# One bias row per quarter spread by a shuffle, and another order at the end of routing

## The chip, the cores and the metric

The kernel runs on one NeuronCore of a Trainium2 chip. The metric is the device time of one execution in microseconds; lower is better. A core has five engines that run their own instruction streams and meet at semaphores: TensorE (PE), VectorE (DVE), ScalarE (ACT), GpSimd (POOL) and SyncE (SP, which here only issues transfers). All transfers run on the core's 16 DMA engines.

## The reference

One decoder layer on 1024 tokens of width 1024: adaLN modulation, a gated MLP mixer beside a sparse attention, then a mixture of experts, then a final norm. The change lies in the mixture of experts and in the routing ahead of it:

```python
def moe(h, w_router, b_router, w_gu, b_gu, w_dn, b_dn):
    ...
    logits = (hf @ w_router + b_router).astype(jnp.float32)
    top_logits, top_idx = lax.top_k(logits, TOP_K)          # 4 of 32 experts
    wts = jax.nn.softmax(top_logits, axis=-1)
    ...
    def expert_block(args):
        xb, e = args
        gu = xb @ w_gu[e] + b_gu[e]
        x_glu = jnp.minimum(gu[:, 0::2], SWIGLU_LIMIT)
        x_lin = jnp.clip(gu[:, 1::2], -SWIGLU_LIMIT, SWIGLU_LIMIT)
        act = x_glu * jax.nn.sigmoid(SWIGLU_ALPHA * x_glu) * (x_lin + 1.0)
        return act @ w_dn[e] + b_dn[e]
    ...
```

All data are float32. An expert's weights are 8 MB (gate and up) and 4 MB (down).

## The kernel before

**Stages.** The first 600 us hold the modulation, the projections and the attention. From about 601 us the routing stage walks over 8 tiles of 128 tokens: output projection, residual, norm, transpose, router logits, top 4, and the place of each (token, expert) pair in a list in DRAM (`list_d`), written by indirect transfers of POOL (`scatter`). In the trace this is L1188 to L1520.

**Experts.** From about 738 us the experts run. The tokens of an expert are cut into blocks of 32 (`BLK`). The 128 partitions hold a block four times: partition q*32 + r stands for quarter q of the columns and row r of the block. `up` (L1701) multiplies a block by the gate-and-up weights in two halves h (5 and 3 of 8 column tiles), `gates` (L1754 to L1764, DVE, with the activation of ACT, L1748, in its midst) makes the gated product and transposes it into `actT`, `down` (L1713) multiplies by the down weights, `weigh` (L1776, L1780) adds the down bias and the token's weight. POOL fetches the next block's rows (`gather`, L1650) and adds a finished block to the result in DRAM (`add_rows`, L1659). A block takes PE about 10.4 us.

**Order of the experts.** Experts are placed by their counts from the first tiles: `SEGMENTS` runs through a large expert's first half, a small expert, the large one's second half, for 8 pairs, then 16 middling experts one after another: 40 segments, 143 blocks in all. Every engine reads a segment's number of blocks from memory and loops.

**Weights.** `expert_loads` has SP load each expert in 12 pieces into a ring that holds two experts. A piece is issued when the same piece of the expert two places before is spent and at most `UNDER_WAY` = 4 pieces are under way. Where blocks are many, the ring waits for PE; where they are few, PE waits for the ring.

**Biases.** `b_e` are two tiles of 128 x 768: a quarter's gate, up and down biases (768 numbers) are needed on the 32 partitions of that quarter. `load_bias` has ACT's queue load four transfers of 32 partitions, each reading one row of DRAM 32 times: 4 x 96 KB an expert, 12.6 MB in all. Experts use the two tiles in turn, and a tile is loaded when the expert that used it is through.

**End of routing.** Blocks 0 and 1 (`FIRST` = 2) are known after 4 tiles and are gathered early. After the last tile POOL scatters the last pairs, loads the first expert's whole list (`load_rows`, four transfers of 32 partitions with the same 32 rows), adds block 0 to the result, takes the ids (`take_rows`), gathers block 2, loads the second expert's list, and enters its loop, whose first gather is block 3. PE does `up` of block 0 between the last tiles' products, waits for `halves` (DVE's count of blocks by expert), then does both parts of `down` of block 0, then block 1. DVE does the gates of block 0 after the last places.

## Time and profile before

| what | us |
|---|---|
| median of 3 runs | 2314.43 (2310.81 to 2315.14) |
| the profiled execution's own time | 2316.25 |
| its span, first to last instruction | 2314.4 |
| PE busy | 2200.6 (95%) |
| DVE / POOL / ACT busy | 1029.5 / 849.1 / 333.1 |
| moved by DMA | 534.03 MB, 498.27 MB of it read from HBM |

The profile lists groups of instructions, waits and timelines. "Idle before" is the time in which an engine stood still ahead of an instruction, with the event that ended it. A row of a timeline merges instructions of one line; in brackets stands the idle time ahead of it. PE's ends are modelled. TensorE's clock has two levels, 1.2 and 2.4 GHz; the granted clock is given as a share of the upper one.

### The profile page before, as it was taken

What the parts mean: (1) busy time and instruction counts of PE and PEld (TensorE: products, weight loads), DVE (VectorE), ACT (ScalarE), POOL (GpSimd) and SP (SyncE); (2) the same over time, 40 slices, a digit from 0 to 9 for tenths busy, and PEclk for the clock granted to TensorE, in tenths of its full rate; (3) what the DMA queues carried; (4) which work ended last, traced back from release to release, by engine and by line L of the source; (5) the groups of instructions that cost most, each with busy time, mean ns of one, the idle gap of its engine ahead of it and who ended that gap; (6) DMA issues with size and microseconds to landing.
All of it is one profiled execution on the core that took longest, in us unless ns stands there. A gap on an engine that the chain in (4) does not pass through costs nothing.

```text
span 2314.4 us, 80327 instructions
## 1 busy us (share of the span) xinstructions
PE 2200.6 (95%) x31685; PEld 1502.2 (65%) x31685; DVE 1029.5 (44%) x3487; ACT 333.1 (14%) x919; POOL 849.1 (37%) x1658
## 2 busy tenths in 40 slices
PE   6999989999899899999999999999999999999995
PEld 2777776666544467777777777767675567775573
DVE  2464237777255434343434343434443344443344
ACT  0000017777211000000000000000000000000001
POOL 2011006554224443434343434344443344443433
PEclk9999998999999999999999999999999999999998
DMA  9531051000336787686768686878979978989996
GB/s 312 191 137 58 12 158 35 1 2 1 116 107 229 275 289 250 218 282 224 274 220 287 215 286 213 289 253 276 380 250 355 377 272 317 381 305 390 390 379 224
DMA packets 183488, 534.03 MB, mean 231 GB/s; under 512 B 30152, under 2 KB 59216, under 8 KB 183248
## 3 DMA queue, kind: packets, MB, share of 16 engines
q1 hardware_dynamic: 143472, 479.09, 55.7%
q0 software_dynamic: 33360, 39.96, 8.2%
q10 hardware_dynamic: 6480, 12.72, 1.9%
q8 instruction: 99, 1.62, 0.3%
q14 instruction: 77, 0.63, 0.1%
HBM read 498.27 MB, written 33.34 MB: 230 GB/s over the span
## 4 chain that ended last, share of the span: by engine, by line
PE 55%; DMA 14%; issue 2%; SPq 1%; POOL 1%; DVE 1%; POOLq 0%; another core or an unknown queue 0%; ACT 0%; DVEq 0%; ACTq 0%
PE psum L1701 34%; PE psum L1713 17%; DMA w_ring<-in_w_gate_up 8%; DMA w_ring<-in_w_down 4%; PE psum L1259 4%; DMA x_gathered<-h_rows,scalars_i 1%; SPq L1583 0%; DVE x L1399 0%; POOL slot_list L1214 0%; DMA x<-x_rows 0%; PE psum L1268 0%; DMA token<-k_pairs 0%; SPq L1145 0%; DMA x_rows<-y_out,scalars_i 0%; SPq L1608 0%
## 5 line engine op out<-in xcount | busy, mean ns | idle before, releaser
L1701 PE MATMUL psum<-w_ring,xT 128*32 128x320 f32 (+1 forms) x18304 | 1023.7, 381 | 19.2 <-issue 14.7
L1701 PEld LDWEIGHTS psum<-w_ring,xT 128*32 128x32 f32 x18304 | 696.6, 110 | 340.7 <-issue 41.5
L1713 PE MATMUL psum<-w_ring,actT 128*32 128x256 f32 x9152 | 531.0, 382 | 17.3 <-DMA w_ring<-in_w_down 15.7
L1713 PEld LDWEIGHTS psum<-w_ring,actT 128*32 128x32 f32 x9152 | 349.8, 111 | 152.6 <-DMA w_ring<-in_w_down 20.7
L1642 POOL TENSOR_TENSOR scalars<-scalars 128x1 f32<-128x1 f32 x575 | 108.9, 189 | 728.8 <-DVE xT L1768 562.6
L1754 DVE TENSOR_TENSOR glu<-psum,expert_bias 128x160 f32<-128x160 f32 (+1 forms) x286 | 83.1, 291 | 537.8 <-PE psum L1701 537.7
L1748 ACT ACTIVATE glu<-glu 128x160 f32<-128x160 f32 (+1 forms) x286 | 88.7, 310 | 1444.3 <-DVE glu L1756 1429.7
L1659 POOL DMA_INDIRECT x_rows<-y_out,scalars_i x142 | 228.0, 1606 | 47.2 <-issue 46.9
L783 POOL TENSOR_SCALAR scores<-scores,coef 128x64 f32<-128x64 f32 (+5 forms) x128 | 134.1, 1063 | 137.5 <-DVE coef L992 137.5
L1650 POOL DMA_INDIRECT x_gathered<-h_rows,scalars_i x144 | 153.3, 1064 | 81.3 <-issue 79.2
L1776 DVE TENSOR_TENSOR psum<-psum,expert_bias 128x256 f32<-128x256 f32 x143 | 61.8, 432 | 242.2 <-PE psum L1713 223.4
L906 ACT ACTIVATE scores<-scores,nmax 128x64 f32<-128x64 f32 (+8 forms) x192 | 114.5, 600 | 15.3 <-DVE nmax L977 15.0
L1780 DVE SCALAR_TENSOR_TENSOR y_out<-psum,scalars,gate_q 128x256 f32<-128x256 f32 x143 | 69.1, 483 | 76.9 <-DMA x_rows<-y_out,scalars_i 63.5
L977 DVE CUSTOM_DVE_ANT_0 scores<-psum,attn_tables 128x512 f32<-128x512 f32 (+4 forms) x192 | 81.5, 462 | 38.3 <-PE psum L831 38.0
L849 PEld LDWEIGHTS psum<-ident,scores 128*128 128x128 f32 (+1 forms) x592 | 62.5, 139 | 49.0 <-issue 41.2
L1764 DVE STREAM_TRANSPOSE actT<-lin 128x160 f32<-128x160 f32 (+1 forms) x286 | 89.2, 312 | 10.0
L849 PE MATMUL psum<-ident,scores 128*128 128x128 f32 (+1 forms) x592 | 90.4, 286 | 0.9 <-ACT probT L915 0.6
L1762 DVE SCALAR_TENSOR_TENSOR lin<-lin,glu 128x160 f32<-128x160 f32 (+1 forms) x286 | 83.6, 292 | 11.2 <-ACT glu L1748 0.7
L831 PE MATMUL psum<-kT_all,q_negated 64*128 64x512 f32 (+3 forms) x384 | 84.4, 522 | 1.4 <-DVE nmax L977 0.6
L329 POOL TENSOR_TENSOR vms<-vms,eps 128x8 f32<-128x8 f32 x8 | 5.6, 706 | 215.7 <-DVE vms L582 215.7
L1620 POOL DMA_DIRECT2D slot_rows<-slot_list x128 | 67.3, 541 | 43.5 <-issue 43.5
L915 ACT COPY probT<-psum 128x512 f32<-128x512 f32 (+1 forms) x136 | 74.2, 572 | 55.4 <-PE psum L849 45.0
(246 smaller groups left out, 1882.7 us busy)
## 6 DMA issues: line engine op xcount, KB each, us to landing
w_ring<-in_w_gate_up SPq DMA_DIRECT2D x128, 1280.0 KB
w_ring<-in_w_down SPq DMA_DIRECT2D x128, 1024.0 KB
w_ring<-in_w_gate_up SPq DMA_DIRECT2D x128, 768.0 KB
ada_then_cmp_in<-in_w_ada SPq DMA_DIRECT2D x16, 1024.0 KB, 6.3
expert_bias<-bias_by_quarter ACTq DMA_DIRECT2D x128, 96.0 KB
ada<-in_w_ada SPq DMA_DIRECT2D x8, 1024.0 KB, 5.6
xt<-in_x SPq DMA_DIRECT2D x8, 512.0 KB, 6.3
w_uv_then_w_out<-in_w_in SPq DMA_DIRECT2D x4, 1024.0 KB, 9.5
```

Of the source, the lines that this page charges most:

```text
L783: nc.gpsimd.tensor_scalar(rows, rows, coef[qt % 2][:, col:col + 1], None, ALU.mult).then_inc(s_sl, 1)
L831: last = nc.tensor.matmul(psA[at % 2][g][:, col:col + m], qn[qt % 2][half(g), j, :], keys, start=True, stop=True)
L849: last = nc.tensor.transpose(psT[at % 2][0:m, (2 * t + g) * P:(2 * t + g + 1) * P], score[n % (LAG + 1)][g][:, c0:c0 + m], ident[:])
L906: nc.scalar.activation(rows, rows, ACT.Exp, scale=-1.0, bias=nmax[qt % 2][:, col:col + 1], accum_out=sums[qt % 2][:, col:col + 1]).then_in ...
L1259: last = nc.tensor.matmul(psO[n], mix, wo[:, k, n * 512:(n + 1) * 512], start=(k == 0), stop=(k == KD - 1))
L1642: nc.gpsimd.tensor_tensor(tick[:], zero[:], zero[:], ALU.add).then_inc(s_steps, 1)
L1650: nc.gpsimd.indirect_dma_start(xg[:], None, h2_q, bass.IndirectOffsetOnAxis(ap=ids_x[:], axis=0), bounds_check=4 * (SEQ + BLK) - 1, oob_is ...
L1659: nc.gpsimd.indirect_dma_start(x1_q, bass.IndirectOffsetOnAxis(ap=ids_y[:], axis=0), y_out[:], None, compute_op=ALU.add).then_inc(s_ysc, 16)
L1701: last = nc.tensor.matmul(psU[h][j * BLK:(j + 1) * BLK, :], xT[:, k, :], w[:, j], start=(k == 0), stop=(k == KD - 1))
L1713: last = nc.tensor.matmul(psO[m * BLK:(m + 1) * BLK, :], actT[h][:, i, :], w[:, m * Q:(m + 1) * Q], start=(k == 0), stop=(k == KD - 1))
L1748: nc.scalar.activation(glu[:, 0:n], glu[:, 0:n], ACT.Gelu_apprx_sigmoid).then_inc(s_gate[h], 1)
L1764: nc.vector.transpose(actT[h][:].rearrange("p k q -> p (k q)"), lin[h][:]).then_inc(s_actT[h], 1)
```

## The change

It has these parts. (1) `load_bias` loads one row to the first partition of each quarter, 4 x 3 KB, and a new `spread_bias` has DVE copy it to the other 31 partitions by one STREAM_SHUFFLE over 128 x 768 in place, once an expert: before the loop of the expert's first segment, and for expert 0 in the routing stage. Both tiles are cleared once by POOL. (2) The list rows come in one transfer to 128 partitions, whose source names the 32 rows four times, in place of four transfers. (3) POOL computes the address of the first expert's list ahead of the last scatter, and gathers block 2 ahead of adding block 0. (4) DVE and ACT do the first half of block 0's gates right after the loop over tiles, and PE its part of `down` ahead of the `halves` products.

```diff
                 parts.gather(pool, 1, 4)
         tiles(pool, body)
         scatter(TILES - 2, 0)
+        lines = parts.lines_of(pool, 0)
         scatter(TILES - 1, 1)
         for i in range(2):
             pool.wait_ge(s_sc[i], 16 * TOPK * TILES // 2)
             pool.wait_ge(s_xnst[i], 16 * TILES // 2)
-        parts.load_rows(pool, 0)
+        parts.load_lines(pool, 0, lines)
         pool.wait_ge(s_spare, 48)
         for i in range(2):
             pool.wait_ge(s_x1st[i], 16 * TILES // 2)
-        parts.add_rows(pool, 0, 7)
         parts.take_rows(pool, 0)
         pool.wait_ge(parts.s_ids, 4)
-        parts.gather(pool, 2, 10)
+        parts.gather(pool, 2, 7)
+        parts.add_rows(pool, 0, 10)
         parts.load_rows(pool, 1)
         pool.wait_ge(s_order, 3)
         expert_rows(pool, parts)
...
         places(TILES - 1, 1)
 
         nc.tensor.matmul(psR[0:E, E:E + 2], total_b[0][:], ones[:, 0:2], start=True, stop=True).then_inc(s_cnt, 1)
+        pe.wait_ge(parts.s_actT[0], 1)
+        parts.down(pe, 0, 0)
         pe.wait_ge(s_halves, 1)
         for i in range(2):
             last = nc.tensor.matmul(psR[0:1, P + i * E:P + (i + 1) * E], halves[:, i:i + 1], select[0:E, :], start=True,
                                     stop=True)
         last.then_inc(s_cnt, 1)
-        parts.down_both(pe, 0, 0)
+        pe.wait_ge(parts.s_actT[1], 1)
+        parts.down(pe, 0, 1)
         pe.wait_ge(parts.s_xT, 3)
         parts.up(pe, 0, 0)
         parts.up(pe, 0, 1)
...
             if back:
                 weights(t - 1, 1 - par)
         tiles(act, body)
+        parts.activation(act, 0, 0)
         copy_h2(TILES - 1, 1)
         copy_logits(TILES - 1)
         weights(TILES - 1, 1)
-        for b in range(FIRST):
-            parts.activations(act, b)
+        parts.activation(act, 0, 1)
+        parts.activations(act, 1)
         act.wait_ge(s_order, 3)
         expert_activations(act, parts)
         final_squares(act, final)
...
             if t == KNOWN_TILES + 1:
                 place_experts()
         tiles(dve, body)
+        parts.spread_bias(dve, 0)
+        parts.gates(dve, 0, 0, 0)
         assign(TILES - 2, 0)
         choose(TILES - 1, 1)
         assign(TILES - 1, 1)
...
         nc.vector.tensor_scalar(none[:], key[0:1, 0:1].to_broadcast([1, N_SEGMENTS]), 0.0, None, ALU.mult)
         with nc.allow_low_precision("whole numbers up to 16"):
             nc.vector.tensor_reduce(halves[:], over[:].rearrange("p (j i) -> p i j", i=2), AX.X, ALU.add).then_inc(s_halves, 1)
-        dve.wait_ge(parts.s_bias[0], 64)
-        parts.gates(dve, 0, 0, 0)
         parts.gates(dve, 0, 1, 0)
         parts.transpose_x(dve, 1)
         dve.wait_ge(s_cnt, 4)
...
         which = pool.value_load(order[0:1, e:e + 1], min_val=0, max_val=E - 1)
         return list_v[bass.ds(which, 1)].rearrange("a t l -> (a t) l")
 
+    def load_lines(pool, e, lines):
+        pool.dma_start(rows_f[e % 2][:].rearrange("p b c -> p (b c)"), lines.partition_broadcast(4)).then_inc(s_rows, 16)
+
     def load_rows(pool, e):
-        lines = lines_of(pool, e)
-        for q in range(4):
-            pool.dma_start(rows_f[e % 2][q * BLK:(q + 1) * BLK, :, :].rearrange("p b c -> p (b c)"), lines
-                           ).then_inc(s_rows, 16)
+        load_lines(pool, e, lines_of(pool, e))
 
     def load_first_rows(pool):
         lines = lines_of(pool, 0)
-        for q in range(4):
-            pool.dma_start(rows_f[0][q * BLK:(q + 1) * BLK, 0:FIRST, :].rearrange("p b c -> p (b c)"), lines[:, 0:2 * FIRST]
-                           ).then_inc(s_rows, 16)
+        pool.dma_start(rows_f[0][:, 0:FIRST, :].rearrange("p b c -> p (b c)"), lines[:, 0:2 * FIRST].partition_broadcast(4)
+                       ).then_inc(s_rows, 16)
 
     def clear(pool):
         nc.gpsimd.memset(zero[:], 0.0).then_inc(s_clear, 1)
...
         nc.gpsimd.memset(xg[:], 0.0).then_inc(s_xT, 1)
 
         nc.gpsimd.memset(tick[:], 0.0).then_inc(s_steps, 1)
-        pool.wait_ge(s_clear, 3)
+        for i in range(2):
+            nc.gpsimd.memset(b_e[i][:], 0.0).then_inc(s_clear, 1)
+        pool.wait_ge(s_clear, 5)
         pool.wait_ge(s_c, 16)
 
     def carry_waits(pool, done):
...
                                      compute_op=ALU.add).then_inc(s_ysc, 16)
 
     def take_first_rows(pool):
-        pool.wait_ge(s_rows, 64)
+        pool.wait_ge(s_rows, 16)
         nc.gpsimd.tensor_tensor(rows_f[0][:, 0:FIRST, 0], rows_f[0][:, 0:FIRST, 0], quarter[:, 0:1].to_broadcast([P, FIRST]), ALU.add
                                 ).then_inc(s_quarter, 1)
         pool.wait_ge(s_quarter, 1)
...
             skip = skip + FIRST
         pool.wait_ge(s_ids, 2 * g + 2)
         if part != 1:
-            pool.wait_ge(s_rows, 64 * (e + 2))
+            pool.wait_ge(s_rows, 16 * (e + 2))
             nc.gpsimd.tensor_tensor(rows_f[e % 2][:, :, 0], rows_f[e % 2][:, :, 0], quarter[:, 0:1].to_broadcast([P, EDGES]), ALU.add
                                     ).then_inc(s_quarter, 1)
         pool.wait_ge(s_quarter, e + 2)
...
             act.wait_ge(s_y, blocks)
         rows = bias_d.rearrange("(e q) n -> e q n", q=4)[bass.ds(which, 1)].rearrange("a q n -> (a q) n")
         for q in range(4):
-            act.dma_start(b_e[at][q * BLK:(q + 1) * BLK, :], rows[q].partition_broadcast(BLK)
-                          ).then_inc(s_bias[at], 16)
+            act.dma_start(b_e[at][q * BLK:q * BLK + 1, :], rows[q:q + 1, :]).then_inc(s_bias[at], 16)
+
+    def spread_bias(dve, p):
+
+        at = HALF_OF[p]
+        turn = sum(HALF_OF[q] == at for q in range(p + 1))
+        dve.wait_ge(s_bias[at], 65 * turn - 1)
+        nc.vector.stream_shuffle(b_e[at][:], b_e[at][:], mask=[0] * BLK).then_inc(s_bias[at], 1)
+        dve.wait_ge(s_bias[at], 65 * turn)
 
     def load_gate(act):
         for q in range(4):
...
                                                                             ).partition_broadcast(BLK)
                           ).then_inc(s_g, 16)
 
+    def activation(act, b, h):
+        act.wait_ge(s_glu[h], b + 1)
+        n = ACT_TILES[h] * BLK
+        nc.scalar.activation(glu[:, 0:n], glu[:, 0:n], ACT.Gelu_apprx_sigmoid).then_inc(s_gate[h], 1)
+
     def activations(act, b):
         for h in range(2):
-            act.wait_ge(s_glu[h], b + 1)
-            n = ACT_TILES[h] * BLK
-            nc.scalar.activation(glu[:, 0:n], glu[:, 0:n], ACT.Gelu_apprx_sigmoid).then_inc(s_gate[h], 1)
+            activation(act, b, h)
 
     def gates(dve, b, h, at):
         n, first, end = ACT_TILES[h] * BLK, 2 * BLK * ACT_FROM[h], 2 * BLK * (ACT_FROM[h] + ACT_TILES[h])
...
         b = parts.first_of(dve, g)
         many = parts.many_of(dve, g)
         dve.wait_ge(parts.s_ids, 2 * g + 4)
-        e = SEGMENTS[g][0]
+        e, part = SEGMENTS[g]
         at = HALF_OF[e]
-        dve.wait_ge(parts.s_bias[at], 64 * sum(HALF_OF[p] == at for p in range(e + 1)))
+        if g and part != 1:
+            parts.spread_bias(dve, e)
         with dve.Fori(0, many) as i:
             n = b + i
             parts.gates(dve, n, 0, at)
```

A last hunk, left out here, only makes the new functions known to the callers.

How instructions stand on DVE after the loop over tiles, before (weights of the last tile but one, `wts`, then its places, `prod` and `rank_f`; the waits in brackets name semaphores):

```order
L1424 CAST mask_b<-mask 128x32
L1426 RECIPROCAL winv<-wsum 128x1 [waits wexp_ready]
L1427 TENSOR_SCALAR wts<-wexp,winv 128x4 [waits dve_chain3]
L1433 TENSOR_TENSOR prod<-hot,psum 128x128 [waits place_ps,dve_chain3]
L1434 TENSOR_REDUCE rank_f<-prod 128x4 [waits dve_chain3]
L1435 CAST rank<-rank_f 128x4 [waits dve_chain3]
```

and in the change:

```order
L1431 RECIPROCAL winv<-wsum 128x1 [waits wexp_ready]
L1432 TENSOR_SCALAR wts<-wexp,winv 128x4 [waits dve_chain3]
L1747 STREAM_SHUFFLE expert_bias<-expert_bias 128x768 [waits expert_bias_loaded0,dve_chain3]
L1770 TENSOR_TENSOR glu<-psum,expert_bias 128x160 [waits w_spent3,expert_bias_loaded0]
L1772 TENSOR_SCALAR glu<-glu 128x160 [waits gates_chain]
L1773 TENSOR_TENSOR lin<-psum,expert_bias 128x160
L1775 TENSOR_SCALAR lin<-lin 128x160 [waits gates_chain]
L1778 SCALAR_TENSOR_TENSOR lin<-lin,glu 128x160 [waits gate_ready0,gates_chain]
L1780 STREAM_TRANSPOSE actT<-lin 128x160 [waits gates_chain]
L1438 TENSOR_TENSOR prod<-hot,psum 128x128 [waits place_ps]
L1439 TENSOR_REDUCE rank_f<-prod 128x4 [waits dve_chain3]
```

The shuffle and six instructions of the gates of block 0 now stand between the weights and the places.

ACT at the same place, before, from the last residual's square (`sq`) to the first activation (`glu`):

```order
L1354 ACTIVATE sq,ms_1<-x 128x1024 [waits rstd3_ready,ms3_ready,x1_ready]
L1368 ACTIVATE wexp,wsum<-below_top 128x4 [waits neg_top_ready]
L1359 COPY h2T<-psum 128x512 [waits xnT_ps]
L1359 COPY h2T<-psum 128x512
L1364 COPY logitsT_parts<-psum 128x128 [waits logitsT_ps]
L1368 ACTIVATE wexp,wsum<-below_top 128x4 [waits neg_top_ready]
L1748 ACT_TABLE_LOAD
L1748 ACTIVATE glu<-glu 128x160 [waits glu_ready0]
L1748 ACTIVATE glu<-glu 128x96 [waits glu_ready1]
```

and in the change:

```order
L1358 ACTIVATE sq,ms_1<-x 128x1024 [waits rstd3_ready,ms3_ready,x1_ready]
L1372 ACTIVATE wexp,wsum<-below_top 128x4 [waits neg_top_ready]
L1760 ACT_TABLE_LOAD
L1760 ACTIVATE glu<-glu 128x160 [waits glu_ready0]
L1363 COPY h2T<-psum 128x512 [waits xnT_ps]
L1363 COPY h2T<-psum 128x512
L1368 COPY logitsT_parts<-psum 128x128 [waits logitsT_ps]
L1372 ACT_TABLE_LOAD
L1372 ACTIVATE wexp,wsum<-below_top 128x4 [waits neg_top_ready]
L1760 ACT_TABLE_LOAD
L1760 ACTIVATE glu<-glu 128x96 [waits glu_ready1]
```

The first activation, with a table load, stands ahead of the copy of the last tile's transposes (`h2T`), and two more table loads have come in.

POOL from the load of the first expert's list (`slot_rows`) on, before:

```order
L1620 DMA slot_rows<-slot_list 32x64 x4
L1642 TENSOR_TENSOR scalars<-scalars 128x1 [waits y_sb,x1_stored1,index_steps,x1_stored0,spare_rows_set]
L1657 TENSOR_TENSOR scalars_i<-row_ids,scalars_i 128x1
L1642 TENSOR_TENSOR scalars<-scalars 128x1 [waits index_steps]
L1659 DMA x_rows<-y_out,scalars_i 4224x256
L1681 TENSOR_TENSOR slot_rows<-slot_rows,quarter 128x32 [waits slot_rows_loaded,ids_ready]
L1684 CAST row_ids<-slot_rows 128x14 [waits quarter_added]
L1685 COPY slot_weights<-slot_rows 128x14
L1642 TENSOR_TENSOR scalars<-scalars 128x1 [waits index_steps,xT_ready,ids_ready]
L1648 TENSOR_TENSOR scalars_i<-row_ids,scalars_i 128x1
L1642 TENSOR_TENSOR scalars<-scalars 128x1 [waits index_steps]
L1650 DMA x_gathered<-h_rows,scalars_i 128x256
```

and in the change:

```order
L1623 DMA slot_rows<-slot_list 128x1x64
L1687 TENSOR_TENSOR slot_rows<-slot_rows,quarter 128x32 [waits ids_ready,x1_stored1,slot_rows_loaded,x1_stored0,spare_rows_set]
L1690 CAST row_ids<-slot_rows 128x14 [waits quarter_added]
L1691 COPY slot_weights<-slot_rows 128x14
L1648 TENSOR_TENSOR scalars<-scalars 128x1 [waits index_steps,xT_ready,ids_ready]
L1654 TENSOR_TENSOR scalars_i<-row_ids,scalars_i 128x1
L1648 TENSOR_TENSOR scalars<-scalars 128x1 [waits index_steps]
L1656 DMA x_gathered<-h_rows,scalars_i 128x256
L1648 TENSOR_TENSOR scalars<-scalars 128x1 [waits index_steps,y_sb]
L1663 TENSOR_TENSOR scalars_i<-row_ids,scalars_i 128x1
L1648 TENSOR_TENSOR scalars<-scalars 128x1 [waits index_steps]
L1665 DMA x_rows<-y_out,scalars_i 4224x256
```

The gather of block 2 (`x_gathered`) now comes ahead of the addition of block 0 to the result (`x_rows`), the load of the list is one transfer to 128 partitions, and the load of the second expert's list follows the addition in place of the gather.

## Rows read from the trace of the kernel before

**Rows 1.** Waits of PE in 1740:1755, 1820:1833, 2080:2092, 2120:2163 (us, times, longest)

```profile
PE psum L1713 <- DMA w_ring<-in_w_down: 3.3, 2, 1.9
...
PE psum L1713 <- DMA w_ring<-in_w_down: 3.9, 2, 2.6
...
PE psum L1713 <- DMA w_ring<-in_w_down: 3.7, 2, 2.1
...
PE psum L1713 <- DMA w_ring<-in_w_down: 4.6, 3, 1.6
```

**Rows 2.** Timeline of PE, the first products after three of those waits

```profile
1752.29 7.09 PE L1701 MATMUL psum<-w_ring,xT 128*32 128x320 f32 x128
...
1831.41 8.74 PE L1701 MATMUL psum<-w_ring,xT 128*32 128x320 f32 x128
...
2090.13 9.08 PE L1701 MATMUL psum<-w_ring,xT 128*32 128x320 f32 x128
```

**Rows 3.** Timeline of SP, where three unbroken stretches of weight loads begin

```profile
1707.52 22.25 SPq L1608 DMA_DIRECT2D w_ring<-in_w_gate_up  x8
...
1784.89 22.86 SPq L1608 DMA_DIRECT2D w_ring<-in_w_gate_up  x8
...
2044.05 23.39 SPq L1608 DMA_DIRECT2D w_ring<-in_w_gate_up  x8
```

**Rows 4.** Timeline of ACT, bias loads inside those stretches

```profile
1739.11 1.76 ACTq L1734 DMA_DIRECT2D expert_bias<-bias_by_quarter  x4
...
1817.21 2.87 ACTq L1734 DMA_DIRECT2D expert_bias<-bias_by_quarter  x4
...
2146.01 1.84 ACTq L1734 DMA_DIRECT2D expert_bias<-bias_by_quarter  x4
```

**Rows 5.** DMA queues in the window 2044:2160 us (packets, MB, share of 16 engines)

```profile
q1 hardware_dynamic: 9951, 38.57, 87.1%
...
q10 hardware_dynamic: 768, 1.57, 4.7%
```

**Rows 6.** Timeline of DVE about the start of a segment at 1063 us

```profile
1068.05 0.33 DVE L1754 TENSOR_TENSOR glu<-psum,expert_bias 128x160 f32<-128x160 f32 x1 [3.73 <-PE psum L1701]
...
1069.56 0.35 DVE L1764 STREAM_TRANSPOSE actT<-lin 128x160 f32<-128x160 f32 x1
...
1072.09 0.40 DVE L1768 STREAM_TRANSPOSE xT<-x_gathered 128x256 f32<-128x256 f32 x1
```

**Rows 7.** Timeline of POOL at the start of the routing stage

```profile
606.63 0.10 POOL L1195 MEMSET eps_nhalf<- 128x1 f32 x1 [3.05 <-DMA quarter<-k_quarter]
```

**Rows 8.** Timeline of DVE at the end of routing

```profile
748.38 0.29 DVE L1433 TENSOR_TENSOR prod<-hot,psum 128x128 f32<-128x128 f32 x1 [3.07 <-PE psum L1293]
...
756.86 0.29 DVE L1433 TENSOR_TENSOR prod<-hot,psum 128x128 f32<-128x128 f32 x1 [3.26 <-remote]
```

**Rows 9.** Timeline of ACT at the end of routing

```profile
746.53 1.07 ACT L1359 COPY h2T<-psum 128x512 f32<-128x512 f32 x2 [2.83 <-PE psum L1268]
...
751.74 1.28 ACT L1748 ACT_TABLE_LOAD   x1
```

**Rows 10.** Timeline of POOL at the end of routing

```profile
768.03 2.07 POOL L1620 DMA_DIRECT2D slot_rows<-slot_list  x4 [3.78 <-issue]
...
771.99 0.92 POOL L1681 TENSOR_TENSOR slot_rows<-slot_rows,quarter 128x32 f32<-128x32 f32 x1
...
774.73 1.09 POOL L1650 DMA_INDIRECT x_gathered<-h_rows,scalars_i  x1 [0.56 <-issue]
...
782.52 1.09 POOL L1650 DMA_INDIRECT x_gathered<-h_rows,scalars_i  x1 [0.56 <-issue]
```

**Rows 11.** The chain that ended last, POOL's address load (start, us)

```profile
766.77 0.31 POOLq L1614
```

**Rows 12.** Timeline of PE from the end of routing on

```profile
759.51 0.21 PE L1330 MATMUL psum<-select,half_counts 32*1 32x32 bf16 x2 [5.84 <-DVE half_counts L1500]
...
790.08 7.12 PE L1701 MATMUL psum<-w_ring,xT 128*32 128x320 f32 x128 [0.85 <-DVE xT L1768]
```

2 lines of the change are left out of this document (added).

## Prediction

> **What bounds the kernel now.** I read the page first: PE is busy 95% of the span, so time is to be had only where PE stands still. So I took the waits of PE from 790 us on. Up to 1700 us the only wait for data is one of 0.85 us, at 790.08 [rows 12]. After that PE waits for the pieces of the down weights in four places: 3.3, 3.9, 3.7 and 4.6 us, 15.5 us in all [rows 1]. Next come the products that follow: 128 products take 7.09 us after the first wait, but 8.74 and 9.08 us after the second and third [rows 2], so there the clock's fall costs 1.6 and 2.0 us more.
>
> Then the timeline of SP: its weight loads run without a gap from 1707.52, from 1784.89 and from 2044.05 us, each time released by PE [rows 3]. The first stretch ends at the first wait, the second at the second, the third holds the third and fourth waits. In such a stretch whatever else the DMA engines carry delays the last piece, and PE with it. The bias loads are such a thing: two are issued in each of the first two stretches (the second ones at 1739.11 and 1817.21) and four in the third, the last at 2146.01 [rows 4], all ahead of the wait that ends the stretch. The DMA queues in 2044:2160 show their part: q10, which carries only them, moved 1.57 MB and took 4.7% of the 16 engines' time [rows 5].
>
> The other place is the end of routing. PE gets block 3 only at 790.08, 0.85 us after it was free [rows 12]; the chain to it runs over DVE's last places, POOL's last scatter, the list rows, and the gathers at 774.73 and 782.52 [rows 10].
>
> **The biases, what is saved.** One expert's biases take 4.7% of 116 us over 4 = 1.36 us of all DMA engines. By bytes it is less: 0.39 MB at q1's rate (87.1% of 116 us for 38.57 MB, 2.62 us/MB) is 1.03 us [rows 5]. After the change 4 rows in place of 128 move, one part in 32. The shares of the queues add up to over 100%, so the first figure is a little high; I take 1.2 us per expert, bounds 1.03 and 1.36.
>
> First stretch: 2 x 1.2 = 2.4 of the 3.3 us. Second: 2.4 of the 3.9, and with 1.5 us left I also take back the 1.6 us of the clock, as 3.3 us of waiting in two pieces cost no clock at 1752.29 [rows 2]: 4.0. Third: 4 x 1.2 = 4.8 of 8.3; the 2.0 us of clock are not added, since they lie between two waits for the same unbroken stretch: what PE gains there it waits at the next. Stretches begin when PE has spent a piece, so an earlier PE shifts the next stretch along and the gains add up. Sum 2.4 + 4.0 + 4.8 = **11.2 us**; bounds 8.2 (1.03, no clock) and 12.5 (1.36, with it). Elsewhere the DMA engines wait for PE, and fewer bytes give nothing.
>
> **The shuffle, what it costs.** 31 segments get one, ahead of DVE's wait for PE. The trace has no shuffle. The nearest row is a transpose, 0.40 us for 256 elements a partition and 0.35 for 160 [rows 6]: 768 elements are at least 0.40 + 512 x 0.52 ns = 0.67 us, at most 3 x 0.40 = 1.2 us. I take 1.0. It costs nothing: DVE stands still 3.73 us at the start of a segment until PE's first half of `up` is done [rows 6]. Part of those are its two address loads; the first instruction of such a load takes 0.31 us on POOL [rows 11], so some 2 us of cover are left. Without the cover it is 31 us. What is queued behind it is the segment's first gates, for which ACT and then PE's `down` wait; the next gather's transpose comes only after them. The bias rows are issued a segment or more ahead, as before. The Trainium skill, "VectorE: DVE Perf Modes", the perf-mode table, gives a shuffle about 2400 ns for 2048 elements, so 0.9 us here as its estimate; no row shows one.
>
> Clearing the two bias tiles adds two memsets to POOL at the stage's start, where it stands still 3.05 us for a constant anyway [rows 7]: nothing.
>
> **The end of routing.** (a) DVE is free at 745.31 (748.38 less its idle 3.07) [rows 8]. The shuffle ends at 746.3, two operations like the 0.33 us of [rows 6] end at 746.95, and the activation, taken as one more of them, at 747.3. ACT now does it ahead of copying the last tile's transposes, which started at 746.53 [rows 9]. That copy feeds the logits, the last places and the last scatter: **+0.8 us** on the whole chain. DVE's own places, waited for until 748.38, are hardly late. The two added table loads are 1.28 us each [rows 9]; the one ahead of the exponential has the logits' product and DVE's reduction as cover: nothing. (b) The list's address is known before the last scatter: the load it saves begins with 0.31 us [rows 11]; I take -0.5 for both instructions and what hangs on them. (c) Four issues of 2.07 us together become one. A quarter is 0.52, an indirect issue for 128 rows 1.09; I take 0.8: -1.3. (d) The list landed at most 1.9 us after the last issue ended (770.10 to 771.99) [rows 10]. Its 128 pieces now hang on one transfer. I take +0.5, bounds 0 and a second 1.9. So the gather of block 2 moves by 0.8 - 0.5 - 1.3 + 0.5 = -0.5 us. PE is there in time: half of block 0's `down` now fills the 5.84 us that PE stood still before 759.51 [rows 12].
>
> But block 3 decides. Between the two gathers POOL now also has the addition of block 0 (1.9 us, it stood ahead of 771.99 [rows 10]), one issue for four (-1.3) and again the landing (+0.5): its gather moves by -0.5 + 1.9 - 1.3 + 0.5 = **+0.6 us**, PE's 790.08 too. Both of PE's gains ahead of it turn into waiting. SP's first loads of expert 1 wait for that addition as well and begin later; blocks of expert 0 cover them. Bounds: -0.9 with the cheap ends, +4.0 with the dear ones. Below that lies one more: at 756.86 DVE ends a wait of 3.26 us whose releaser the profile doesn't know [rows 8], in the midst of this chain. If it doesn't come again, 3.3 us less: -4.2.
>
> For (d) a rule speaks against the change. The row shows only a list spread over 32 partitions by transfer. The Trainium skill, "DMA: Bandwidth & Descriptors", rules for kernel authors, says that an outermost dimension that repeats the source c times confines a transfer to at most c DMA engines: here 4. By it the landing would be near the dear end at both lists.
>
> **Sum.** -11.2 + 0.6 = -10.6 us. The profiled execution took 2316.25 us, which gives 2305.65. It lies 1.8 above the median of the runs shown, 2314.43, so I forecast 2303.8.
>
> **Rivals.**
> 1. *The bias rows sit on one DMA engine.* A piece is ready when the slowest engine is. Before, 768 packets for four experts were 12 an engine and expert [rows 5]; 4 rows of 3 KB in packets of 2 KB (1.57 MB over 768) are 8 packets. All on one engine save it only 4 of 12, 0.4 us an expert: 0.8 + 0.8 + 1.6 - 0.6 = 2.6 us, 2311.8. For it: a transfer with one partition has nothing to be spread by. Against: the row may be cut.
> 2. *Nothing is saved*, since the same row read 32 times was cheap and the weights are held up elsewhere: 2315.0. Against: q10's share of engine time [rows 5] is dearer per byte than q1's.
> 3. *The lists land late*, both by the dear ends: -11.2 + 4.0 = -7.2, 2307.2. The skill's rule above is this rival's.
> 4. *The unexplained wait doesn't come again*: -10.6 - 3.3, 2300.5.
> 5. *Slower: the shuffle is not covered.* Place: a segment's start on DVE. It decides when shuffle and address loads last over 3.73 us. Were all of it on the path: +31 - 10.6, 2334.8. Against: that idle time is three times the dearest shuffle [rows 6].
>
> **Chances.** Forecast 0.50, rivals 0.15, 0.07, 0.15, 0.08, 0.05. What a measurement of this kernel tells from no change is about 0.2%, 4.6 us. The forecast, rivals 3 and 4 are faster by more, of rival 1 a fifth: 0.76. Same: 0.19. Slower: 0.05. Range 2297.5 (12.5 + 4.2 saved) to 2312.5 (rival 1 and a late list).
>
> **What would show it.** Right: q10's share in the late stretches is near nothing, the four waits shrink from 15.5 to about 6 us, the products after 1831 us take 7.1 us, the STREAM_SHUFFLE lasts 1.0 us and DVE still waits after it, the last `h2T` copy starts 0.8 us later, block 3 at about 790.7. Wrong: waits as long as before with q10 empty (rivals 1, 2), a second gather after 785 us (3), block starts that slip at every new expert (5).

## The result, and the profile after

The changed kernel takes 2296.32 us (median of 6 runs, 2292.22 to 2301.77), the kernel before 2313.44 (6 runs): ratio 0.9925, 95% interval 0.9914 to 0.9935. It is faster by 17.1 us where 10.6 were forecast, and lies 1.2 us below the range. The profiled execution took 2299.49 us (span 2297.6).

**The late stretches.** Waits of PE after the change in 1690:1760, 1760:1860, 2020:2100 and 2100:2170 us, which answer to [rows 1] (us, times, longest):

```profile
PE psum L1707 <- issue: 0.7, 2, 0.4
...
PE psum L1719 <- DMA w_ring<-in_w_down: 0.8, 1, 0.8
...
PE psum L1719 <- DMA w_ring<-in_w_down: 1.0, 1, 1.0
...
PE psum L1719 <- DMA w_ring<-in_w_down: 4.5, 3, 1.6
```

The first place has no wait for data left (its 0.7 us are of another kind, marked "issue"), the second and third have shrunk from 3.9 and 3.7 us, and the fourth is as long as before. Next come the products after the second and third place, and the last of the three waits of the fourth:

```profile
1821.21 7.09 PE L1707 MATMUL psum<-w_ring,xT 128*32 128x320 f32 x128
...
2074.50 7.09 PE L1707 MATMUL psum<-w_ring,xT 128*32 128x320 f32 x128
...
2142.13 1.93 PE L1719 MATMUL psum<-w_ring,actT 128*32 128x256 f32 x16 [1.47 <-DMA w_ring<-in_w_down]
```

7.09 us answer to 8.74 and 9.08 in [rows 2]; in 1820:1833 and 2085:2100 the granted clock was 0.80 and 0.77 before, and is 1.00 after. The clock had cost more than that: in the kernel before, 16 products of the down product behind the waits ran slowly too, 1.94 us where 1.07 is the full pace:

```profile
1827.18 1.28 PE L1713 MATMUL psum<-w_ring,actT 128*32 128x256 f32 x16 [2.62 <-DMA w_ring<-in_w_down]
1829.70 1.94 PE L1713 MATMUL psum<-w_ring,actT 128*32 128x256 f32 x16 [1.24 <-DMA w_ring<-in_w_down]
...
2088.42 1.94 PE L1713 MATMUL psum<-w_ring,actT 128*32 128x256 f32 x16 [1.63 <-DMA w_ring<-in_w_down]
```

The DMA queues of the changed kernel in 2044:2160 us (packets, MB, share of 16 engines), against [rows 5]: q10 went from 4.7% to nothing, q1 carries 3.45 MB more in the same time.

```profile
q1 hardware_dynamic: 11001, 42.02, 92.1%
...
q10 hardware_dynamic: 32, 0.05, 0.1%
```

The price of a bias load is best read from SP, which in the third stretch issues without a gap, so that from one expert's first load to the next's is what an expert costs the DMA engines. First load of the stretch and of the fourth expert behind it, before (the first is in [rows 3]) and after:

```profile
2185.59 2.85 SPq L1608 DMA_DIRECT2D w_ring<-in_w_gate_up  x2
```

```profile
2032.14 22.33 SPq L1613 DMA_DIRECT2D w_ring<-in_w_gate_up  x8
...
2167.84 19.77 SPq L1613 DMA_DIRECT2D w_ring<-in_w_gate_up  x7
```

Before (2185.59 - 2044.05) / 4 = 35.4 us per expert, after (2167.84 - 2032.14) / 4 = 33.9: 1.46 us per load, where 1.2 was taken and 1.36 was the upper bound. In the rest of this text "the expert's period" is this number.

**Where the time went.** The start of each block after against before: 2.6 us earlier at block 4, 2.0 to 2.1 from block 30 to block 93, 5.7 behind the first stretch's wait, 11.9 behind the second, 17.6 behind the third, 17.6 behind the fourth, 18.0 at the last. So 15.9 us lie in the late stretches (3.7 + 6.0 + 5.8, and 0.4 elsewhere), 2.0 ahead of them; the kernel's end gives 1.2 back.

**Block 0.** Behind the 2.0 us stands a gain that nobody looked for, where a bias load meets the gather of block 0. ACT issues expert 1's biases at 727.15 before and at 726.59 after, and POOL the gather at 730.96 and 730.37. DVE's transpose of the gathered rows and PE's first products of block 0, before, then after:

```profile
737.75 0.45 DVE L1768 STREAM_TRANSPOSE xT<-x_gathered 128x256 f32<-128x256 f32 x1 [0.59 <-DMA x_gathered<-h_rows,scalars_i]
738.25 6.20 PE L1701 MATMUL psum<-w_ring,xT 128*32 128x320 f32 x64 [2.41 <-DVE xT L1768]
```

```profile
736.55 0.44 DVE L1784 STREAM_TRANSPOSE xT<-x_gathered 128x256 f32<-128x256 f32 x1
737.04 4.51 PE L1707 MATMUL psum<-w_ring,xT 128*32 128x320 f32 x64 [1.73 <-DVE xT L1784]
```

Before, DVE waits 0.59 us for the rows; after, they are there. PE's wait is 0.7 us shorter, and the same 64 products take 1.7 us less: the granted clock in 738.3:744.3 was 0.72, and is 1.00 after. Together that is 2.4 us. All 20 kernels of this study side with their bias load: from the start of these products to PE's next operation it is 4.4 us in the ten that load one row or 192 B pieces, and 6.1 to 6.5 us in the ten that load more.

**The shuffle**, at the start of a segment (idle time ahead of a row in brackets), and as a group:

```profile
1062.88 1.03 DVE L1747 STREAM_SHUFFLE expert_bias<-expert_bias 128x768 f32<-128x768 f32 x1
1065.65 0.33 DVE L1770 TENSOR_TENSOR glu<-psum,expert_bias 128x160 f32<-128x160 f32 x1 [1.74 <-PE psum L1707]
...
L1747 DVE STREAM_SHUFFLE expert_bias<-expert_bias 128x768 f32<-128x768 f32 x32 | 33.4, 1045 | 0.3
```

**The end of routing**, POOL, then PE, DVE and ACT (idle time ahead of a row in brackets):

```profile
762.21 0.78 POOL L1623 DMA_DIRECT2D slot_rows<-slot_list  x1 [2.41 <-DMA slot_list<-pairs,slot]
764.81 0.39 POOL L1687 TENSOR_TENSOR slot_rows<-slot_rows,quarter 128x32 f32<-128x32 f32 x1 [1.83 <-DMA slot_rows<-slot_list]
...
766.84 1.12 POOL L1656 DMA_INDIRECT x_gathered<-h_rows,scalars_i  x1 [0.55 <-POOL scalars L1648]
...
769.82 1.41 POOL L1623 DMA_DIRECT2D slot_rows<-slot_list  x1
775.07 0.23 POOL L1687 TENSOR_TENSOR slot_rows<-slot_rows,quarter 128x32 f32<-128x32 f32 x1 [3.84 <-DMA slot_rows<-slot_list]
...
777.34 1.10 POOL L1656 DMA_INDIRECT x_gathered<-h_rows,scalars_i  x1 [0.55 <-issue]
...
747.50 0.64 PE L1278 MATMUL psum<-h2T,w_router_sb 128*32 128x128 f32 x16 [3.34 <-ACT h2T L1363]
...
785.20 9.36 PE L1707 MATMUL psum<-w_ring,xT 128*32 128x320 f32 x128 [4.39 <-DVE xT L1784]
...
752.19 0.29 DVE L1438 TENSOR_TENSOR prod<-hot,psum 128x128 f32<-128x128 f32 x1
...
746.15 0.34 ACT L1760 ACTIVATE glu<-glu 128x160 f32<-128x160 f32 x1 [2.29 <-DVE glu L1772]
746.39 1.05 ACT L1363 COPY h2T<-psum 128x512 f32<-128x512 f32 x2
```

The gather of block 2 comes 7.9 us earlier (766.84 for 774.73), that of block 3 only 5.2 (777.34 for 782.52). DVE's wait of 3.26 us without a known releaser [rows 8] is absent at 752.19. PE runs ahead over blocks 0 to 2 and then stands still 4.39 us for block 3, and the product behind takes 9.36 us in place of 7.12 [rows 12]: of the 8.4 us won at block 2, 2.6 are left at block 4.

### The profile page after: what moved, and what is told of

The parts are those of the page before. It is cut to its first block, busy times and chain, and to the rows that moved or that the text cites. A ratio compares the mean times of both kernels' runs of the same rounds, so it can differ in the third digit from the quotient of the medians.

```text
span 2297.6 us, 80188 instructions
## 1 busy us (share of the span) xinstructions
PE 2194.2 (96%) x31685; PEld 1501.2 (65%) x31685; DVE 1062.1 (46%) x3551; ACT 335.5 (15%) x921; POOL 807.2 (35%) x1561
## 4 chain that ended last, share of the span: by engine, by line
PE 58%; DMA 11%; issue 1%; SPq 1%; POOL 1%; DVE 1%; POOLq 0%; ACT 0%; DVEq 0%; ACTq 0%
PE psum L1707 36%; PE psum L1719 18%; DMA w_ring<-in_w_gate_up 7%; PE psum L1260 4%; DMA w_ring<-in_w_down 3%; POOL slot_list L1214 0%; DVE x L1404 0%; SPq L1588 0%; DMA slot_rows<-slot_list 0%; DMA x<-x_rows 0%; DMA x_gathered<-h_rows,scalars_i 0%; PE psum L1269 0%; DMA token<-k_pairs 0%; SPq L1145 0%; DMA x_rows<-y_out,scalars_i 0%
## 5 line engine op out<-in xcount | busy, mean ns | idle before, releaser
L783 POOL TENSOR_SCALAR scores<-scores,coef 128x64 f32<-128x64 f32 (+5 forms) x128 | 134.1, 1063 | 137.5 <-DVE coef L992 137.5
L1773 DVE TENSOR_TENSOR lin<-psum,expert_bias 128x160 f32<-128x160 f32 (+1 forms) x286 | 81.0, 283 | 0.0
## 6 DMA issues: line engine op xcount, KB each, us to landing
w_ring<-in_w_down SPq DMA_DIRECT2D x128, 1024.0 KB, 10.4
```

Source lines behind the costliest of these rows:

```text
L783: nc.gpsimd.tensor_scalar(rows, rows, coef[qt % 2][:, col:col + 1], None, ALU.mult).then_inc(s_sl, 1)
```

## The experiments

All were timed against the kernel before on the same chip. One line each; the edits follow (waits of semaphores that go with an edit are left out). Every ratio has its own kernel before, whose median lay between 2313.3 and 2315.3 us. "16 pieces of 192 B", "16 copies, 8 partitions apart" and "16 different rows, neighbouring" compute another result: they leave biases out or add wrong ones.

```
kernel                                     median us  ratio   95% interval      expert's period
bias change alone                          2291.96    0.9899  0.9886 to 0.9911  33.4
all but the bias change                    2318.97    1.0020  1.0011 to 1.0028  35.8
list in four transfers                     2295.27    0.9920  0.9907 to 0.9933  33.8
16 copies of a row                         2316.25    1.0016  1.0005 to 1.0027  35.4
second transfer, 31 copies                 2682.26    1.1581  1.1560 to 1.1602
second transfer, 31 different rows         2680.00    1.1573  1.1553 to 1.1592
POOL's old order                           2294.47    0.9913  0.9897 to 0.9929  33.5
old order of PE, ACT and DVE               2295.56    0.9920  0.9904 to 0.9936  33.9
second transfer, 16 different rows         2324.39    1.0049  1.0033 to 1.0065  35.3
second list early                          2293.39    0.9912  0.9898 to 0.9926  33.9
second list early, engines' old order      2295.00    0.9920  0.9907 to 0.9933  33.6
four shuffles                              2349.53    1.0152  1.0137 to 1.0167
one transfer of 128 rows                   2371.10    1.0246  1.0231 to 1.0262
16 pieces of 192 B per quarter             2299.86    0.9938  0.9924 to 0.9952  33.9
4 copies of a row                          2300.65    0.9947  0.9932 to 0.9962  34.2
bias change and one transfer per list      2294.32    0.9915  0.9903 to 0.9928  33.7
16 copies, 8 partitions apart              2305.78    0.9960  0.9946 to 0.9973  34.7
16 different rows, neighbouring            2316.80    1.0011  1.0002 to 1.0020  35.3
```

### Bias and routing apart

The bias change alone (against the kernel before):

```diff
-            act.dma_start(b_e[at][q * BLK:(q + 1) * BLK, :], rows[q].partition_broadcast(BLK)
-                          ).then_inc(s_bias[at], 16)
+            act.dma_start(b_e[at][q * BLK:q * BLK + 1, :], rows[q:q + 1, :]).then_inc(s_bias[at], 16)
...
-        dve.wait_ge(parts.s_bias[0], 64)
+        parts.spread_bias(dve, 0)
         parts.gates(dve, 0, 0, 0)
```

> Only the bias rows and the shuffle are changed against the kernel before; the lists and the order at the end of routing are as before. Theory A (the biases are worth more than the 11.2 us of the prediction: all 15.9 us by which the block starts shift at the three late stretches hang on them): 2313.4 - 15.9 = 2297.5 us. Rival B (the biases give the 11.2 us forecast, and the other 4.7 us at the stretches come from the lists, which cost one issue on POOL per expert in place of four and one transfer in place of four): 2302.2 us, and the waits of PE for w_down after 1700 us keep about 5 us more than in the changed kernel. Rival C (the two changes help each other only together): above 2305 us.

2291.96 us, 21.7 faster than its kernel before (2313.62) and 4.4 faster than the whole change, with intervals that don't meet. Theory A's sign was right and its size too small; B and C fall. Its four waits after 1700 us are 0, 0, 0 and 3.6 us. The last is the only one left:

```profile
PE psum L1715 <- DMA w_ring<-in_w_down: 3.6, 3, 1.8
```

The same edit taken back in the changed kernel:

> The changed kernel with the bias loads of before and no shuffle: the lists and the end of routing alone. Theory A: it loses the 15.9 us again, 2296.3 + 15.9 = 2312.2 us, with four waits for w_down of together about 15 us after 1700 us and the products at half clock behind the second and third. Rival B: 2296.3 + 11.2 = 2307.5 us, with the waits about 4 to 5 us shorter than before. The prediction's own figure for this part was slower by 0.6 than before, so 2314.0 us; the block starts up to block 93 say 2 us faster.

2318.97 us: slower than before by 0.1 to 0.3%, so the rest of the change is no gain but a loss of 4.4 us with the bias change and 5.4 without it. Theory A's 2312.2 is passed, B falls.

```diff
-        pool.dma_start(rows_f[e % 2][:].rearrange("p b c -> p (b c)"), lines.partition_broadcast(4)).then_inc(s_rows, 16)
+        for q in range(4):
+            pool.dma_start(rows_f[e % 2][q * BLK:(q + 1) * BLK, :, :].rearrange("p b c -> p (b c)"), lines
+                           ).then_inc(s_rows, 16)
```

> The changed kernel with each list loaded by four transfers of 32 partitions as before; everything else as changed. Theory A: only the end of routing moves: four issues for one cost 1.3 us before each of the two gathers, the landing is up to 1.4 us shorter (2.35 in place of 3.84 us at the second list), so between 0 and +2 us: 2296.3 to 2298.5 us, and no waits for w_down come back after 1700 us. Rival B: 4.7 us of the waits come back: 2301 to 2303 us. By the landing's dear end (the one transfer costs more than the four issues it saves) it is faster than the changed kernel by up to 1 us.

2295.27 us: as the changed kernel within the intervals, so no gain or loss of the one transfer for four is seen; the intervals leave room for 2 us either way.

### What a bias load costs by

```diff
-            act.dma_start(b_e[at][q * BLK:q * BLK + 1, :], rows[q:q + 1, :]).then_inc(s_bias[at], 16)
+            act.dma_start(b_e[at][q * BLK:q * BLK + 16, :], rows[q].partition_broadcast(16)).then_inc(s_bias[at], 16)
```

> The changed kernel with each bias row loaded to 16 partitions of its quarter in place of 1 (before: 32), the shuffle unchanged: half of the bytes and descriptors of before. If the cost goes by the bytes (theory A), half of the 15.9 us comes back: 2296.3 + 8.0 = 2304.3 us; by the prediction's 11.2 us half is 5.6: 2301.9 us. If the pieces of w_down have slack first (a wait begins only when the slack is used up) it is less than half: about 2299 to 2301 us, with the first stretch's wait near 1 us and no products at half clock. If the shuffle and not the bytes mattered, or if one row's four transfers sat on one DMA engine and were a cost themselves, 2296.3 or less.

2316.25 us: half of the bytes cost nearly all of it (19.9 of 22.7 us). The prediction's price, which goes by the bytes or the packets' own time, falls here. The trace has each DMA packet with its time, which led to the next idea: the weight packets beside a load are slower while it runs.

The next two kernels keep the one-row load and add a second transfer per quarter:

```diff
             act.dma_start(b_e[at][q * BLK:q * BLK + 1, :], rows[q:q + 1, :]).then_inc(s_bias[at], 16)
+            act.dma_start(b_e[at][q * BLK + 1:(q + 1) * BLK, :], rows[q].partition_broadcast(BLK - 1)).then_inc(s_bias[at], 16)
```

The second kernel has `bias_d[q * BLK:(q + 1) * BLK - 1, :]` as the source.

> The changed kernel with a second transfer per quarter that fills its other 31 partitions with copies of the same bias row, 8 transfers per expert; the shuffle writes over them, so the result is the same and the bytes are those of before again. Theory H (a row that many DMA engines read at the same time slows the packets of the weights beside it: 253 to 278 ns for a weight packet of 5120 B in the 4 us after a bias load begins, against 200 ns else): as with the loads of before, 2316 to 2321 us, with such packets again at 250 ns and more. Theory by bytes alone: 2296.3 + 11 to 16 = 2307 to 2312 us.

> The same as the kernel beside it, but the 31 partitions of a quarter get 31 different rows of the bias tensor (fixed ones), so bytes, packets and transfers are equal and only the addresses differ. Theory H: what is left is the packets' own time, 124 of about 0.12 us over 16 engines = 0.95 us per expert against some 2.0 for the copies, so about half the loss: 2304 to 2309 us, and weight packets of 5120 B stay near 205 ns during the load. Theory by bytes or packets: the same time as the kernel beside it, within 2 us.

2682 and 2680 us, some 385 slower than the changed kernel; no theory had this, and the runs say nothing on copies. ACT's timeline at the end of a segment shows the cause:

```profile
859.28 0.24 ACTq L1741 DMA_DIRECT2D expert_bias<-bias_by_quarter  x1
859.68 7.50 ACTq L1740 DMA_DIRECT2D expert_bias<-bias_by_quarter  x1
867.27 0.50 ACTq L1741 DMA_DIRECT2D expert_bias<-bias_by_quarter  x1
869.30 0.34 ACT L1761 ACTIVATE glu<-glu 128x160 f32<-128x160 f32 x1 [17.26 <-issue]
```

The seventh issue of an expert takes 7.50 us, and ACT's engine stands still for 17.26 us ahead of the activation behind it, which the block's down product needs. Each transfer of 31 rows has one 4-byte packet (its signal) in the trace, where those of 16 and of 32 rows have 16. The Trainium skill, "DMA: Bandwidth & Descriptors", "Why a DMA increments its semaphore by 16 and not by 1", says that as many DMA engines take part as the largest number up to 16 that divides the slowest dimension of both sides, and that each posts a signal; the trace agrees: 31 rows, one signal; 16 rows, 16. By that rule all 31 rows went through one engine.

```diff
             act.dma_start(b_e[at][q * BLK:q * BLK + 1, :], rows[q:q + 1, :]).then_inc(s_bias[at], 16)
+            act.dma_start(b_e[at][q * BLK + 16:(q + 1) * BLK, :], bias_d[q * BLK:q * BLK + 16, :]).then_inc(s_bias[at], 16)
```

> The changed kernel with a second transfer per quarter that brings 16 different rows of the bias tensor to 16 of its other partitions; the shuffle writes over them. Transfers, packets and bytes are those of the kernel that loads the same row to 16 partitions (2316.3 us), and 16 rows spread over 16 engines (31 rows sat on one and cost 386 us), but no row is read twice. Theory H (one row read by 16 engines at once is what is dear, for its own packets, 177 ns against 125, and for the weight packets beside it, 285 to 333 ns against 205): only the packets' own time is left, 64 of 0.125 us and as many of 0.01 over 16 engines = 0.54 us per expert against 1.8, so about 0.3 of the 20 us: 2300 to 2304 us, weight packets of 5120 B near 205 to 220 ns during the load. Theory by bytes or packets: 2314 to 2318 us.

2324.39 us; not the 2300 to 2304 of theory H. But it holds a second cause: with eight issues ACT stands still 18 times, for up to 10.4 us, without a wait that the profile knows (166 us in all, none in the changed kernel), and blocks slip there, mostly by 0.5 to 1 us. Only the late stretches count for the question: 35.3 us per expert, as with copies. H is in doubt.

> The changed kernel with one bias transfer per expert, which brings each of the 4 rows to the 32 partitions of its quarter (one transfer of 128 rows; bytes as before the change, one issue in place of four; the shuffle changes nothing then). Theory K (a bias load costs by transfers times the DMA engines each uses: 64 such pairs before and with 16 rows, 4 now): 16 pairs, a quarter of the loss, 2296.3 + 5 = about 2301 us, 34 to 34.3 us per expert in the late stretches. Theory B (by bytes, but on the busiest engine or with a floor that 16 rows already reach): 2314 to 2318 us as before, 35.4 us per expert.

```diff
-        for q in range(4):
-            act.dma_start(b_e[at][q * BLK:q * BLK + 1, :], rows[q:q + 1, :]).then_inc(s_bias[at], 16)
+        act.dma_start(b_e[at][:], rows.unsqueeze(1).to_broadcast([4, BLK, 3 * D // 4])).then_inc(s_bias[at], 16)
```

2371.10 us: both theories missed it. One transfer whose slowest dimension is 4 has 4 signals in the trace, so by the same rule 4 engines carry 32 rows each, and PE waits 46.9 us for the down weights after 800 us.

> The changed kernel, but a quarter's transfer brings only the first 48 of the row's 768 numbers, to 16 partitions: the biases of the other columns are left out, so the result is another; transfers, packets and engines are those of the kernel with 16 copies (2316.3 us), the bytes are those of one row. Theory K: the loss is as with 16 copies: 2312 to 2318 us, 35.4 us per expert in the late stretches. Theory B: as the changed kernel or a little above, 2296 to 2299 us, since 64 packets of 192 B take 0.03 us each, 0.15 us per engine with their 4 signals.

```diff
+            act.dma_start(b_e[at][q * BLK:q * BLK + 16, 0:48], rows[q][0:48].partition_broadcast(16)).then_inc(s_bias[at], 16)
```

2299.86 us, 3.5 above the changed kernel, with intervals that meet. As many packets, signals and engines as with 16 copies, and nearly nothing of its 20 us: theory K falls.

> The changed kernel with each bias row loaded to 4 partitions of its quarter in place of 1: 16 packets of 3 KB per expert, on up to 4 engines per transfer. Theory K: 16 pairs, a quarter of the loss: about 2301 us. Theory B by total bytes (4 of 32 rows): 2297 to 2299 us. By a floor that any spread transfer reaches: 2310 us and more.

```diff
+            act.dma_start(b_e[at][q * BLK:q * BLK + 4, :], rows[q].partition_broadcast(4)).then_inc(s_bias[at], 16)
```

2300.65 us, 4.3 above: K's figure, which the run with 192 B pieces has refuted as a reason; theory B's 2297 to 2299 is within the noise as well, and only the floor of 2310 falls. What is left is many engines that move 3 KB each at the same time; nothing between 4 and 16 was tried. The last two runs ask whether reading or writing is dear:

```diff
+            first = 4 * (q % 2) + q // 2
+            act.dma_start(b_e[at][first:first + 121:8, :], rows[q].partition_broadcast(16)).then_inc(s_bias[at], 16)
```

> As the kernel with 16 copies of each bias row (2316.3 us), but the 16 partitions that a transfer writes are 8 apart over the whole tile in place of neighbours. Every quarter then takes the biases of the first, so the result is another; transfers, packets, engines, bytes and the rows read are the same. Theory D (what is dear is the writing into a few neighbouring partitions): 2298 to 2303 us, 33.6 to 34.2 us per expert in the late stretches, weight packets of 5120 B below 240 ns. Theory S (what is dear is that 16 engines read one row at once): 2314 to 2318 us, 35.3 us per expert, weight packets at 285 to 330 ns. If neither matters, 2314 to 2318 us here and in the kernel beside it.

```diff
+            act.dma_start(b_e[at][q * BLK:q * BLK + 16, :], bias_d[q * BLK:q * BLK + 16, :]).then_inc(s_bias[at], 16)
```

> As the kernel with 16 copies of each bias row (2316.3 us), with the same 16 neighbouring partitions, but 16 different rows of the bias tensor (fixed ones) in place of copies, so the biases added are others and the result is another; transfers, packets, engines, bytes and the partitions written are the same. Theory D: 2314 to 2318 us. Theory S: 2298 to 2303 us. The run with 16 different rows and eight transfers speaks for D, but there ACT was held up by the eighth issue.

16 different rows on neighbouring partitions: 2316.80, as 16 copies there (2316.25). What is read doesn't matter; theory S falls. 16 copies on partitions 8 apart: 2305.78, 10.5 us less with as many packets of the same size. Where they are written matters, and theory D holds for about half of the loss. The periods say the same (SP, first load of the stretch and of the fourth expert behind it; 35.4 us with 16 copies on neighbours, 34.7 with them apart):

```profile
2041.59 23.47 SPq L1613 DMA_DIRECT2D w_ring<-in_w_gate_up  x8
...
2183.32 5.88 SPq L1613 DMA_DIRECT2D w_ring<-in_w_gate_up  x3
```

```profile
2037.58 23.40 SPq L1613 DMA_DIRECT2D w_ring<-in_w_gate_up  x8
...
2176.57 12.28 SPq L1613 DMA_DIRECT2D w_ring<-in_w_gate_up  x5
```

From the traces' packets, over 30 bias loads each: the mean of a weight packet of 5120 B in the 4 us from a load's first packet; the load's own packets as time of 16 engines; the slowing, which is the excess of those weight packets over their mean 8 to 2 us ahead of the load, times their number, over 16 engines; and the time against the changed kernel:

```
bias load                          weight packet  own us  slowing us  sum   kernel, us
32 copies (all but bias changed)   261 ns         1.33    0.45        1.8   +22.7
16 copies, neighbouring            308 ns         0.77    0.85        1.6   +19.9
16 different rows, neighbouring    309 ns         0.79    0.88        1.7   +20.5
16 copies, 8 apart                 231 ns         0.57    0.23        0.8    +9.5
4 copies                           221 ns         0.15    0.16        0.3    +4.3
16 pieces of 192 B                 202 ns         0.10    none        0.1    +3.5
1 row (changed kernel)             205 ns         0.03    none        0.03    0
```

Both order the kernels, but only the sum gives the sizes: the first five lose 12 to 14 us for each us of the sum, and 17 to 29 for each us of own time, which would put 16 copies at little over half of 32. The size fits as well: eight loads lie in the late stretches, 8 x 1.8 = 14.4 us, with the clock's 2.7 of the second stretch and 2.4 of block 0 some 19.5 of the 22.7 (an estimate). The Trainium skill, "SBUF — State Buffer", "Door 1: The DMA port swizzle", maps partitions to 16 ports: 32 neighbours reach 8 ports with 4 rows each, 16 neighbours 4 ports with 4 rows each, 16 rows 8 apart 8 ports with 2 rows each. Rows per port so counted are 4 in the first three kernels and 2 in the fourth, as their losses go; 4 copies, 4 rows on one port, fit only with the 4 engines that write them. No run changes the ports alone, so that they are the reason isn't shown.

### The shuffle's cover

```diff
+        for i in range(4):
+            nc.vector.stream_shuffle(b_e[at][:], b_e[at][:], mask=[0] * BLK).then_inc(s_bias[at], 1)
+            dve.wait_ge(s_bias[at], 68 * turn - 3 + i)
```

> The changed kernel with every bias tile shuffled four times in place of once; the three more change no value. One shuffle takes 1.03 to 1.05 us and DVE still stands 1.74 us behind it at a segment's start. If that is the cover, three more (3.1 us) come out 1.4 us late at each of 31 segments: +43 us, 2339 us (2330 to 2345). If the shuffle were already on the path (rival 5 of the prediction), all 3.1 x 31 = 97 us show: 2393 us. If DVE had more room than that idle time, it stays below 2310 us.

2349.53 us, 53.2 above the changed kernel: 1.7 us for each of the 31 segment starts, with 3.1 us more of shuffles. So 1.4 us of cover were left behind the one shuffle, a little less than the idle 1.74. One shuffle is hidden; rival 5 falls.

### What the rest of the change loses

```diff
+        parts.add_rows(pool, 0, 7)
         parts.take_rows(pool, 0)
         pool.wait_ge(parts.s_ids, 4)
-        parts.gather(pool, 2, 7)
-        parts.add_rows(pool, 0, 10)
+        parts.gather(pool, 2, 10)
```

> The changed kernel, but on POOL the addition of block 0 stands ahead of the gather of block 2 again, as before. The kernel with the bias change alone takes 2292.0 us, so the end of routing as changed costs 4.3 us. Theory P (the loss comes from POOL's order: the gather of block 3 is not earlier though that of block 2 is, PE stands still for it and loses clock in the block after, 8.5 to 9.4 us in place of 7.1): PE's idle time is shared over blocks 2 and 3 again, no product at half clock, 2292 to 2294 us. Rival E (it comes from PE, ACT and DVE, who do block 0 ahead): unchanged at 2296 us.

> The changed kernel with the order of PE, ACT and DVE at the end of routing as before (block 0's first gates, activation and half of the down product behind the last tile), POOL as changed. Theory P: PE reaches block 2 later, so less of its idle time falls in one piece before block 3; 2295 to 2297 us. Rival E (doing block 0 early costs the 4.3 us, by the copy on ACT that the logits wait for, 3.3 us of waiting at 747.50, and by the larger hole before block 3): 2292 to 2293 us.

The first has POOL's old order, the second the old order of PE, ACT and DVE: 2294.47 and 2295.56 us. Both lie between the changed kernel and the bias change alone, and their intervals meet both, so neither order can be said to carry the loss by itself. POOL's old order closes the hole before block 3 as theory P says.

```diff
+        parts.load_rows(pool, 1)
         pool.wait_ge(parts.s_ids, 4)
         parts.gather(pool, 2, 7)
         parts.add_rows(pool, 0, 10)
-        parts.load_rows(pool, 1)
```

> The changed kernel, but the list of the second expert is loaded right behind the taking of the first, ahead of the gather of block 2. Theory P (what the change of order at the end of routing costs is the second list's landing behind the addition, 3.84 us of POOL's idle time, and the hole of PE before block 3, 4.39 us with 2.2 us of clock behind it): the gather of block 3 comes some 3 to 4 us earlier (773 to 774 in place of 777.34), block 3 at 781 to 782 with 7.1 us of products: 2296.3 - 4 = 2292 us. If what PE gains there is waited for again later, or if the loss lies elsewhere: 2295 to 2297 us.

> The kernel with the old order of PE, ACT and DVE at the end of routing and POOL as changed (2295.6 us), with the second expert's list also ahead of the gather of block 2. Theory P: no waiting before block 3; block 2 is then the one that decides: 2292 to 2294 us. If the old order of the engines were the better one by itself, this is the fastest of all, below 2291 us. If nothing comes through: 2295 to 2296 us.

> The kernel with the bias change alone (2292.0 us), and each list loaded by one transfer in place of four; the order at the end of routing stays as before the change. If the 3.3 to 4.3 us that the rest of the change costs come from the new order: 2290 to 2292.5 us (two issues of 2.07 us become 0.78, ahead of the gathers of blocks 2 and 3, where PE stood still 1.76 and 0.15 us, so at most 1.9 us faster). If they come from the one transfer per list: 2295 to 2297 us, and the late stretches are longer by 0.3 to 0.6 us per expert.

2293.39, 2295.00 and 2294.32 us: the second list early, the same with the engines' old order, and the bias change with one transfer per list. With the second list early, POOL gathers block 3 at 772.48 and PE has it without any wait:

```profile
769.91 7.11 PE L1707 MATMUL psum<-w_ring,xT 128*32 128x320 f32 x128 [0.15 <-DVE xT L1784]
780.29 7.09 PE L1707 MATMUL psum<-w_ring,xT 128*32 128x320 f32 x128
```

The hole and its clock are cured, and block 3 starts 3.75 us earlier than with the bias change alone (784.04). That lead holds to block 94 and is gone at block 132: it loses 0.8, 1.6 and 1.3 us about the last three of the four waits. POOL's old order loses its lead of 2.5 us there too. So the hole explains what happens at block 3, and not the end time. The bias change alone has the lowest median, but of the kernels with one-row loads only the whole change has an interval apart from its own (four shuffles aside).

## Why the prediction was wrong

**The near hit is partly luck.** 17.1 us were measured for 10.6, 1.2 us outside the range, but the parts were further off, with opposite signs. The bias change alone is worth 21.7 us where 11.2 stood, and the rest costs 4.4 on top of it where 0.6 stood.

**What bounds the kernel: right, with one place missed.** Of the 18 us by which the last block starts earlier, all but 2 lie at the late waits. "Elsewhere the DMA engines wait for PE, and fewer bytes give nothing" is wrong at block 0, where the lighter load gave 2.4 us.

**The price of a load: the step that failed.** "I take 1.2 us per expert, bounds 1.03 and 1.36": it measured 1.46 us in the third stretch. In the first two, from the stretch's first load to the second expert's down loads, 3.6 us (60.18 to 56.63) and 3.9 (61.43 to 57.55) went with two loads, so 1.8 to 1.9 each. With the bias change alone the period is 33.4 for 35.4, 2.0 per load, and its trace gains 3.7, 7.0, 7.0 and 0.9 us at the four places. The prediction took q10's own share of engine time, even with the note that it was "a little high". What failed is that this share is only the load's own time; it leaves out what the load does to the weight packets beside it, 261 ns for 205. That half the bytes cost nearly as much, and that writing apart costs half, shows that the price goes neither by bytes nor by share.

**The clock: right in kind, too small.** In the second stretch the 1.6 us came back, and 1.1 more from slow pieces of the down product, which [rows 2] don't show. In the third stretch the prediction left the 2.0 us out, since PE waits at the next place for what it gains; so it is: the third place gained 5.8 us with the clock's 2.0 in them, the four loads are worth 4 x 1.46 = 5.84, and the fourth wait stayed 4.5 us. By stretch 3.7 + 6.0 + 5.8 = 15.5 us came of 2.4 + 4.0 + 4.8 = 11.2 forecast.

**"The four waits shrink from 15.5 to about 6 us": right**, 6.3. The shares differ, as the fourth kept all of its own.

**The shuffle: right.** 1.00 to 1.07 us, hidden; 1.4 us of cover behind it, where about 1 was implied.

**The end of routing: the second step that failed.** Forecast +0.6. The traces have -2.0, but 3.3 of it come from the wait of rival 4, 0.5 from ahead of the tiles and 2.4 from block 0 (above); without these it is +4.2, beside 4.4 by the medians of the changed kernel and the bias change alone. At block 3 it is +1.3, near the forecast, out of terms that were off:

(a) The copy's start at 746.39, 0.1 earlier than before, hides the most. PE had its transposes done by 742.6, 2.9 us earlier than before (745.5), and the copy, behind the activation that waits for DVE, stood 3.8 us behind them; PE waited 3.34 us for it. With the bias change alone it follows at once and PE doesn't wait:

```profile
743.20 1.07 ACT L1359 COPY h2T<-psum 128x512 f32<-128x512 f32 x2
...
744.67 0.65 PE L1277 MATMUL psum<-h2T,w_router_sb 128*32 128x128 f32 x16
```

So it is in all four kernels with one-row loads and the old order of PE, ACT and DVE; in the five with as light a load, the new order and one shuffle PE waits 3.3 us. (a) costs 3.3 us, and took back what block 0 had gained. The +0.8 holds only where block 0 runs slowly as before: there the copy stands 2.1 us behind the transposes in six kernels, for 1.1 before. (b) POOL stood still 2.41 us ahead of the list's issue and 3.78 before [rows 10], so -1.4 for -0.5. (c) One issue took 0.78 us at the first list, as forecast (0.8), and 1.41 at the second. (d) The first list landed 1.8 us behind its issue (before at most 1.9), the second 3.8 (before 2.35): +0 and +1.5 for the +0.5 forecast; other kernels had 1.9 to 5.9 at the second.

Missed was what follows a hole: that PE runs ahead into a wait of 4.39 us turns, at 785.20, into 2.24 us of clock; the last 0.6 us go between blocks 4 and 30.

**The rivals.** 1, one DMA engine: each one-row transfer has one signal, and it is harmless, since 4 packets of 0.12 us are at most 0.5 us of one engine. Its price rested on packets of 2 KB; the trace has 128 packets of 3 KB and 64 signals of 4 B an expert, so one row was one packet. 2 falls. 3: its +4.0 for the end of routing is near the +4.2 found, by luck: a late list is seen only at the second load, for 1.5 us, and the first list's 1.8 us are no later than before. The Trainium skill's rule on outermost dimensions ("DMA: Bandwidth & Descriptors", rules for kernel authors) agrees with ACT's transfer of 4 x 32 rows (4 signals), and POOL's first list shows no lateness of the kind. 4: the wait is there in 10 of the 20 traces of this study, at this instruction of DVE (for the last tile in eight, for the one before in two), for 2.7 to 3.6 us, with edits of every kind, so no edit is seen to bring or remove it. The kernel before had it in its one trace and the changed kernel not; that is chance as far as the traces tell, and what DVE waits for stays open. 5 falls.

**Open.** The medians of the kernels with any part of the new order or the one-transfer list lie 1.4 to 4.4 us above the bias change alone, and the lead of 0.8 to 3.7 us that four of their traces have at block 93 is lost behind it; why is not settled, and one trace each can't tell 0.4 us per expert from chance. Nor is it shown what in the writing of neighbouring partitions is slow, or whether it counts within one transfer or over the four of an expert.

## What to carry to other kernels

Where a stage is bound by DMA, a small load beside the big ones is not priced by its bytes or its own share: compare how long the big stream's packets take while it runs and when it doesn't, and time from one issue to the same issue a period later. Load a repeated row once and spread it on an idle engine rather than writing it to neighbouring partitions many times; and when loads are cut, choose a slowest dimension that 16 divides. Look too for a small load beside a gather that the next stage waits for: 0.6 us of landing became 2.4 us at block 0. Work that is pulled ahead of an unmoved arrival only joins the holes before it, and here one hole of 4.39 us cost 2.24 us of clock as well. And work put ahead of a step that others wait for costs nothing only while they come late: when PE came 2.9 us earlier, it waited 3.3 us for the copy. A result near the forecast proves no term of it: run the parts apart.

## What the runs showed of the hardware that was not expected

- 16 rows of 3 KB to 16 neighbouring partitions slowed weight packets of 5120 B from 207 ns shortly ahead of the load to 308 ns, the same rows to partitions 8 apart to 231 ns.
- Transfers of 31 rows had one signal each, and eight transfers per expert from ACT then held one issue up for 7.50 us, with 17.26 us of idle time ahead of the next activation.
- A bias load of 4 or more rows a quarter, issued 3.8 us ahead of a gather, went with a slower clock in PE's first products on the gathered rows: 6.1 us for 4.4, and 0.72 for 1.00 in the kernel before.
- A shuffle of 768 elements a partition takes 1.05 us on the mean, against 0.40 for a transpose of 256 [rows 6].
